# Four pairs of projection tiles per head by one level of Strassen's scheme, with quarter sums of x in DRAM

## What is computed

```python
xn = rmsnorm(x, norm_gain)
proj = xn @ w_in                          # (tokens, 1024) x (1024, 4616)
gb, gc, hc, zc, q, k, v, o, zm, ig, fg = split(proj)   # 512 each; ig, fg: 4
yc, conv_new = short_conv(gc * hc, conv_buf, conv_w)   # 3 taps over time
y_conv = gb * yc * silu(zc)
h, state = mlstm(q, k * 128 ** -0.5, v, ig + b_i, log_sigmoid(fg + b_f), state)
h = head_rmsnorm(h) * mh_norm_gain
y_m = h * sigmoid(o) * silu(zm)
out = concat(y_conv, y_m) @ w_out
y = rmsnorm(x + out, final_norm_gain)     # and the new states
```

## Time and profile before

| | |
|---|---|
| time, median of 3 runs | 1104.06 us (1102.57 to 1105.48) |
| span of the profiled execution | 1100.9 us |
| time not in that span, against the median | 3.2 us |
| TensorE busy | 1061.1 us (96%), 7180 matmuls |
| VectorE, ScalarE, GpSimd busy | 540.9, 340.7, 257.9 us |
| DMA | 108.74 MB, mean 99 GB/s |

### The profile page before, as it was taken

How to read it: one execution, slowest core, us unless ns; L and a number is a source line. 1 busy time by engine, 2 the same in 40 slices (tenths; PEclk the granted TensorE clock), 3 DMA queues, 4 the chain that set the end, 5 groups by cost and what they waited for, 6 DMA issues and landing times. The chain is left out here.

```text
span 1100.9 us, 17978 instructions
## 1 busy us (share of the span) xinstructions
PE 1061.1 (96%) x7180; PEld 602.0 (55%) x7180; DVE 540.9 (49%) x1008; ACT 340.7 (31%) x672; POOL 257.9 (23%) x333
## 2 busy tenths in 40 slices
PE   3999999999999999999999999999999999999995
PEld 3655546565666555656665556566655555444442
DVE  5786664556553434575534345655332323434333
ACT  6636434243402232434022324340213131111111
POOL 5012313021211323212113232121111121542422
PEclk9999999999999999999999999999999999999998
DMA  9484532033200322342003224310212062365651
GB/s 243 135 182 78 132 86 49 24 107 101 89 22 17 96 63 77 93 110 89 21 17 96 64 77 120 102 32 22 93 43 86 25 220 91 108 223 205 233 201 77
DMA packets 124184, 108.74 MB, mean 99 GB/s; under 512 B 42384, under 2 KB 109092, under 8 KB 124100
## 3 DMA queue, kind: packets, MB, share of 16 engines
q1 hardware_dynamic: 88192, 68.83, 22.0%
q0 software_dynamic: 7600, 25.03, 6.2%
q10 hardware_dynamic: 28308, 13.73, 4.8%
HBM read 65.43 MB, written 33.41 MB: 90 GB/s over the span
## 5 line engine op out<-in xcount | busy, mean ns | idle before, releaser
L800 PE MATMUL bank<-xTh,Wh 128*128 128x512 f16 (+2 forms) x1304 | 421.2, 342 | 5.7 <-DVE Wl L163 5.7
L801 PE MATMUL bank<-xTl,Wh 128*128 128x512 f16 (+2 forms) x1304 | 423.9, 342 | 0.0
L802 PE MATMUL bank<-xTh,Wl 128*128 128x512 f16 (+2 forms) x1304 | 423.6, 342 | 0.0
L802 PEld LDWEIGHTS bank<-xTh,Wl 128*128 128x128 f16 x1304 | 129.2, 99 | 120.3 <-issue 0.7
L800 PEld LDWEIGHTS bank<-xTh,Wh 128*128 128x128 f16 x1304 | 129.2, 99 | 113.4 <-DVE Wl L163 6.0
L801 PEld LDWEIGHTS bank<-xTl,Wh 128*128 128x128 f16 x1304 | 129.3, 99 | 108.8 <-issue 2.4
L809 PE MATMUL bank<-Wh,xTh 128*128 128x128 f16 x544 | 92.8, 219 | 0.6 <-DVE ysum L163 0.6
L811 PE MATMUL bank<-Wh,xTl 128*128 128x128 f16 x544 | 92.8, 219 | 0.0
L810 PE MATMUL bank<-Wl,xTh 128*128 128x128 f16 x544 | 92.8, 219 | 0.0
L163 ACT ACTIVATE tz<-bank 128x512 f32<-128x512 f32 x32 | 19.1, 598 | 148.4 <-PE bank L802 147.7
L672 POOL TENSOR_TENSOR ysumst<-ysum,ysumst 128x1024 f16<-128x1024 f32 x16 | 34.1, 2130 | 105.5 <-ACT ysumst L163 105.5
(11 more groups left out here) (336 smaller groups left out, 1520.5 us busy)
## 6 DMA issues: line engine op xcount, KB each, us to landing
wst<-in_w_in ACTq DMA_DIRECT2D x23, 512.0 KB, 3.9
xs<-in_x_prompt SPq DMA_DIRECT2D x22, 512.0 KB, 4.3
y_ops<-ysumst POOLq DMA_DIRECT2D x16, 512.0 KB, 3.2
w_ops<-xs SPq DMA_DIRECT2D x16, 448.0 KB, 4.5
wst<-in_w_in SPq DMA_DIRECT2D x13, 512.0 KB, 5.5
out<-xs POOLq DMA_DIRECT2D x11, 512.0 KB, 2.9
Wh<-y_ops SPq DMA_DIRECT2D x12, 448.0 KB, 3.6
Wl<-y_ops SPq DMA_DIRECT2D x12, 448.0 KB, 4.4
```

The lines of the kernel that those rows point to most:

```text
L800: mm(out, wh[:, k, :], xh, start=(k == 0), stop=False)
L801: mm(out, wh[:, k, :], xl, start=False, stop=False)
L802: last = mm(out, wl[:, k, :], xh, start=False, stop=(k == KT - 1))
```

## The change

**Products.** In heads 1 to 3, K and Q, GC and HC, ZC and GB, O and ZM form four pairs. A pair of one block is a 2 x 2 problem: two halves of D (four K tiles each), two tiles, two halves of the block's tokens (256 each). Instead of eight half products, seven are done (strassen_product: 4 K tiles x 3 matmuls of 256 columns), on quarters and on sums of quarters of x and W. Seven weight operands of a pair lie in Wp[p] (OP_11 ... OP_T2), four sums of x quarters of a block in one buffer xsum (X_S2, X_S1, X_S3, X_S4). The products go, in this order, into four slots (half banks of PB0, PB1, T0, N1): first, second, third and fourth slot, then three more that accumulate on top of what VectorE has written back into the first, third and fourth (p1_ready, u4_ready, c22_ready). VectorE does five steps of 256 columns a pair (second_sum, quarter_22, fourth_sum, quarter_12, quarter_21), ScalarE two (first_copied, first_quarter). V stays as it was, and now comes first in a block (values). The mixed tokens' second tile of each pair is made from three operands, 36 matmuls of 80 columns instead of 24. Head 0 is computed tile by tile as before. The 128 ** -0.5 of the keys is now folded into the exponents.

**x.** Head 0 stores the split x of each block to DRAM (store_x, to x_ops); heads 1 to 3 load it per block into one of two regions xreg[0] and xreg[1], one block ahead (load_a). The four sums of a block (high and low parts) are computed once, from rows of x that are loaded again, in eight passes of 512 KB: two in head 0, six in blocks (1,0), (1,1) and (1,2) (SUMS_AT). A pass: rows loaded by SyncE (load_sum_rows), scaled by ScalarE (sums_norm), four sums of 512 on GpSimd (sum_rows), two high halves on ScalarE (sum_rows_high), a low half on VectorE (sum_rows_low), DMA transposes and two stores to x_sums by SyncE (turn_sums). load_sums brings the four sums of the next block (512 KB each) into xsum, at the end of SyncE's list for a block.

**Weights.** load_raw brings the raw tiles of the next head on SyncE's queue (seven in its block 2, two in block 3); VectorE scales them (raw_gain), ScalarE makes high halves (pair_high, pair_sums_high), VectorE and GpSimd low halves (pair_low, pair_sums_low), GpSimd the sums (pair_first_sum, pair_sums).

**Moved.** The slabs of w_out go to blocks (2,1), (2,2), (3,1), (3,2). In VectorE's list sum_rows_low, or the second output_low, is the last of such a block. The output stage loads its operands late, into memory of xreg and Wp that comes free. Several small buffers (gain, junk) share memory.

The core of the diff, all in the engine lists and their helpers:

```diff
+PAIRS = [(K, Q), (GC, HC), (ZC, GB), (O, ZM)]
+NP = len(PAIRS)
+HALF = BT // 2
+W_ORDER = [V, K, Q, GC, HC, ZC, GB, O, ZM]
+OP_11, OP_21, OP_T3, OP_22, OP_T4, OP_T1, OP_T2 = range(7)
+WOPS = 7
+X_S2, X_S4, X_S3, X_S1 = range(4)
+XREG = 2 * KT * BT
 STATES_IN = DB * H + DB * 2 * H
...
+SUMS_AT = {(1, 0): (2, 3), (1, 1): (4, 5), (1, 2): (6, 7)}
...
+            def load_sums(g, b):
+
+                m = v_of(g, b)
+                sp.wait_ge(xq_out, xq_out_0 + (32 * 2 * (b + 1) if g == 1 else 32 * NQ))
+                src = x_sums[b, :, :].rearrange("p (r s h k t) -> p r (s h) k t", r=2, s=2, h=2, k=KT)
+                dst = xsum.rearrange("p r s h k t -> p r (s h) k t")
+                for op, product in ((X_S2, 2), (X_S1, 3), (X_S3, 4), (X_S4, 6)):
+                    if m:
+                        sp.wait_ge(s_prod, 7 * (NP * m - 1) + product)
+                    elif op == X_S2:
+                        sp.wait_ge(tile_done, 3 * NT)
+                    r, k = op // 2, slice(op % 2 * (KT // 2), (op % 2 + 1) * (KT // 2))
+                    sp.dma_start(dst[:, r, :, k, :], src[:, r, :, k, :]).then_inc(xs_in[op], 16)
...
+            for g in range(1, H):
+                for b in range(NB):
+                    m = v_of(g, b)
+                    if m + 1 < (H - 1) * NB:
+                        load_a(*divmod(m + 1 + NB, NB))
+                    for i, q in enumerate(SUMS_AT.get((g, b), ())):
+                        if b == 0 and i == 0:
+                            sp.wait_ge(wt_low, 3)
+                        load_sum_rows(q)
+                        turn_sums(q)
+                    if (g, b) in SLAB_FIRST:
+                        first_slab = SLAB_FIRST[g, b]
+                        for slab in (first_slab, first_slab + 1):
+                            load_slab(slab)
+                        for slab in (first_slab, first_slab + 1):
+                            store_slab(slab)
+                    if g < H - 1 and b == NB - 2:
+                        sp.wait_ge(wt_low, NP * g)
+                        if g == 1:
+                            sp.wait_ge(xq_out, xq_out_0 + 32 * NQ)
+                        else:
+                            sp.wait_ge(wo_out, 32 * SLABS // 2)
+                        load_raw(g + 1, V, K, Q, GC, HC, ZC, GB)
+                    if g < H - 1 and b == NB - 1:
+                        sp.wait_ge(wv_low, wv_low_0 + g + 1)
+                        load_raw(g + 1, O)
+                        sp.wait_ge(wt_low, NP * g + 1)
+                        load_raw(g + 1, ZM)
+                    if m + 1 < (H - 1) * NB:
+                        load_sums(*divmod(m + 1 + NB, NB))
+
+            last = unit_of(H - 1, NB - 1, 0)
             sp.wait_ge(wo_out, 32 * SLABS)
...
+            def pool_heads(g, b):
+                before = divmod(nth(g, b) - 1, NB)
+                ahead = b == NB - 1 and g < H - 1
+                if b == 0:
+                    pair_sums(g, 2)
+                    pair_first_sum(g, 3)
+                    pair_sums_low(g, 2)
+                store_y(*before, 1)
+                y_operands(*before)
+                if b == 0:
+                    pair_sums(g, 3)
+                if ahead:
+                    pair_first_sum(g + 1, 0)
+                if (g, b) in SUMS_AT:
+                    sum_rows(SUMS_AT[g, b][0])
+                store_sums(*before)
+                if b == 0:
+                    pair_sums_low(g, 3)
+                if ahead:
+                    pair_sums(g + 1, 0)
+                if b == 1:
+                    store_states(g)
+                if (g, b) in SLAB_FIRST:
+                    output_sums(SLAB_FIRST[g, b])
+                if b == 0:
                     pool.wait_ge(mx_ms, g + 1)
                     pool.tensor_tensor(hm[:, 4:5], hm[:, 3:4], halves[0:MIX, 0:1], ALU.pow).then_inc(mx_rs, 1)
-                if first and b == 0:
-                    x_power(9)
+                if ahead:
+                    pair_first_sum(g + 1, 1)
+                    pair_sums_low(g + 1, 0)
+                store_y(g, b, 0)
                 if b == 0:
                     store_mixed(g, 0)
-                if b == 1:
-                    pool.wait_ge(mx_states, g + 1)
-                    dst = c_s[:, bass.ds(g, 1), :, :].rearrange("b h d v -> d (b h) v")
-                    pool.dma_start(dst, cs[:, :, 0:P]).then_inc(cs_out, 16)
-                if (g, b) in SLAB_FIRST:
-                    output_sums(SLAB_FIRST[g, b])
-                store_y(g, b, 0)
                 if (g, b) in SLAB_FIRST:
                     output_sums(SLAB_FIRST[g, b] + 1)
-                if first and b == 0:
-                    x_power(10)
-                pool.wait_ge(h_ms, nth(g, b) + 1)
-                pool.tensor_tensor(hrs[:, :], hms[:, :], halves[:, :], ALU.pow).then_inc(h_rs, 1)
+                if ahead:
+                    pair_sums(g + 1, 1)
+                head_power(g, b)
                 if b == 0:
                     store_mixed(g, 1)
+                if (g, b) in SUMS_AT:
...
+            def strassen_product(unit, part_x, op, slot, start):
+
+                p = unit % NP
+                for k in range(KT // 2):
+                    wh, wl = Wp[p][:, op, 0, k, :], Wp[p][:, op, 1, k, :]
+                    mm(slot_bank[slot], wh, part_x(0, k), start=(start and k == 0), stop=False, skip_group_check=not start)
+                    mm(slot_bank[slot], wh, part_x(1, k), start=False, stop=False, skip_group_check=not start)
+                    last = mm(slot_bank[slot], wl, part_x(0, k), start=False, stop=(k == KT // 2 - 1), skip_group_check=not start)
+                last.then_inc(s_prod, 1)
...
+            def pair_block(g, b, p, between):
+
+                unit, m = unit_of(g, b, p), v_of(g, b)
+                x = x_block(g, b)
+                first, second, third, fourth = range(4)
+
+                def quarter(row, half):
+                    return lambda part, k: x[:, part, half * (KT // 2) + k, row * HALF:(row + 1) * HALF]
+
+                def sums(op):
+                    return lambda part, k: xsum[:, op // 2, part, :, op % 2 * (KT // 2) + k, :]
+
+                if b == 0:
+                    pe.wait_ge(wb_low, wb_low_0 + w_pairs(g, p) + 1)
...
+                    pe.wait_ge(wt_low, w_pairs(g, p) + 1)
+                between(0)
+                use_slot(first, unit)
+                strassen_product(unit, quarter(0, 0), OP_11, first, True)
+                between(1)
+                use_slot(second, unit)
+                if p == 0:
+                    pe.wait_ge(xs_in[X_S2], xs_in_0[X_S2] + 16 * (m + 1))
+                strassen_product(unit, sums(X_S2), OP_T2, second, True)
+                between(2)
+                use_slot(third, unit)
+                if p == 0:
+                    pe.wait_ge(xs_in[X_S1], xs_in_0[X_S1] + 16 * (m + 1))
+                strassen_product(unit, sums(X_S1), OP_T1, third, True)
+                between(3)
+                use_slot(fourth, unit)
+                if p == 0:
+                    pe.wait_ge(xs_in[X_S3], xs_in_0[X_S3] + 16 * (m + 1))
+                strassen_product(unit, sums(X_S3), OP_T3, fourth, True)
+                between(4)
+                pe.wait_ge(p1_ready, unit + 1)
+                strassen_product(unit, quarter(0, 1), OP_21, first, False)
+                between(5)
+                pe.wait_ge(u4_ready, unit + 1)
+                if p == 0:
+                    pe.wait_ge(xs_in[X_S4], xs_in_0[X_S4] + 16 * (m + 1))
+                strassen_product(unit, sums(X_S4), OP_22, third, False)
+                between(6)
+                pe.wait_ge(c22_ready, unit + 1)
+                strassen_product(unit, quarter(1, 1), OP_T4, fourth, False)
+                between(7)
+
+            def pe_heads(g, b):
+                n, m = nth(g, b), v_of(g, b)
+
+                def values():
...
+                def values():
+
+                    if b == 0:
+                        pe.wait_ge(wv_low, wv_low_0 + g)
+                    pe.wait_ge(xa_in[m % 2], 16 * (m // 2 + 1))
+                    if m:
+                        pe.wait_ge(slot_free[1], 5 * m)
+                    else:
+                        pe.wait_ge(p_free[1], NT * NB // 2)
+                    for c in range(CH):
+                        last = value_product(PB[1][:, c * P:(c + 1) * P], block_x(g, b, c, c + 1))
+                    last.then_inc(v_done, 1)
...
+                def in_keys(k):
+                    if k == 2:
+                        pe.wait_ge(n_free, n)
+                        pe.wait_ge(s_free, n * 3)
+                        transposed(g, eh, t0(g, b, "hT"))
+                    if k == 3 and b == 1:
+                        states_round(g, b, 1)
+                    if k == 4 and b == 0:
+                        mixed_tile(g, b, K)
+                    if k == 6:
+                        arguments(g, b)
+                    if k == 7 and b == 0:
```

(49 more changed lines are left out.)

1394 lines of the change are left out of this document (1014 added, 380 removed).

## The result

The changed kernel takes 1445.88 us (1442.46 to 1454.95, 4 runs) against 1103.49 us for the kernel before in the same series: 1.3116 times as long, 95% interval 1.3074 to 1.3158. The profiled execution has a span of 1443.7 us. So the change makes the kernel 342 us slower; forecast were 215 us, and the range ended at 1390.

A forecast was written before the change was run, and what follows sets the result against it. TensorE, 96% busy, was taken as the bound. Span 1100.9 - 52.2 array time + 130 x sums + 81.5 head starts + 20 head 0 + 26 clock + 10 contention = 1316.2, forecast 1319 us; range 1195 to 1390.

The forecast's parts named there:

- last term: GpSimd and VectorE contending side by side, plus VectorE's long list before a head's end: 10 us, bounds 0 and 25.
- clock: TensorE falls to half rate after idling: 2 us for each of 13 long waits, 26 us.
- x sums: Seven waits before blocks of heads 1 to 3 for late-loaded x sums: 130 us, bounds 95 and 160.
- last block of head 0: Waits from ScalarE's rows, VectorE's weight loads and sums handed between engines: about 20 us, bounds 5 and 30.
- head starts: TensorE waits in blocks (g,0) for values, mixed K and mixed GC: 81.5 us, bounds 50 and 100.
- Array time: TensorE in heads 1 to 3: 336 matmuls of 256 columns replace 192 of 512 per block; -52.2 us overall.
- the link I named: Head starts: ScalarE's high halves for pairs 2 and 3 precede its copy of values; 17.5 us late, heads 2 and 3.
- As a sum this fits: Plain blocks: VectorE's work rises to about 29 of 46.7 us, ScalarE and GpSimd below half; only order does not fit.
- (c): Rival: lists lock into each other further than followed, each wait moving the next; over 1390, say 1420 us; chance 0.1.
- Output stage: Kernel's end: its weights load during the last two pairs and first products; cost 0, at most 5 us.

The follow-up runs named there:

- Runs 1: Changed kernel with the next block's x sums loaded ahead of the seven weight loads in SyncE's list, blocks (1,2) and (2,2); 1429.45 us against 1445.88.
- runs 2: Changed kernel with the next block's x sums loaded ahead of the second w_out slab's stores, in the four slab blocks; 1391.22 us against 1445.88.
- 3: Changed kernel with the second pass over x left out in (1,0), (1,1), (1,2), results wrong; 1371.6 us against 1445.88.
- run 4: Changed kernel with ScalarE's copies of values and mixed K put ahead of high halves at head starts; 1446.9 us against 1445.88.
- run 9: kernel 7 with VectorE's cn updates earlier and, in (1,1) and (1,2), ScalarE's row scaling later and x sums loaded ahead of rows; 1266.59 us.
- kernel 10: kernel 7 with GpSimd's weight sums and low halves for heads 2 and 3 cut to 2 of 128 columns, results wrong; 1226.5 us.
- run 11: kernel 10 with GpSimd waiting for two 16-byte DMAs ahead of each group of sums and each pair's low halves, results wrong; 1255.52 us.
- kernel 7: Changed kernel with head-start lists reordered, passes earlier in own buffers, x sums ahead of slab stores and weights, V/K gains and head 0 row scaling later; 1273.55 us.
- 8: Changed kernel with dummy 256-column matmuls ahead of each of the seven x-sum waits; 1463.49 us against 1445.88.

## Why the prediction was wrong

The direction was right, and so were the long waits and their places; the size was short by 127 us (1319 against 1446). By the terms of the sum: last term (contention, VectorE's long list) 62 us, clock 33, x sums 18, last block of head 0 8, head starts 6. Point by point:

**Array time: right.** In (3,1) a matmul of 256 columns follows another after 109.2 ns on average (325 steps), forecast 109; 192 of 512 columns at 215.9 gave way to 336: 4.8 us a block. TensorE's busy time shows less of it: without what half clock added (60.4 us after, 1.7 before) it fell by 41 us, from 1059.4 to 1018.5, and in (3,1) from 53.26 to 49.28. A matmul of 256 columns is on record for 0.27 us, while the next can follow after 0.109, so 0.16 us of a wait can lie hidden in busy time. The missing 11 us are short waits, not array time: with every matmul priced at the median step of its form the kernel after has 53 us less.

**x sums: right, somewhat short.** Forecast 20, 21, 34, 10, 25, 10, 10; measured 23.9, 24.5, 37.6, 12.0, 25.9, 12.2, 12.4. Together 148.4 for 130. Runs 1, 2 and 3 take each away by its named cause. What was missing before (1,1): the V tile starts at 411.02, which is T, and GpSimd's power ended at 419.03, so at T + 8.0 and not T + 4.5, in part because VectorE stood 2.7 us at a mixed result that its list has ahead of the means; the rest of the chain, 23.4 us from there to the load's landing, was forecast at 20.8 and 1.4 for the first pass.

**Head starts: right in size, and in the cause only in part.** v 22.6 and 21.5 for 17.5 and 17.5, kfm 3 x 10.5 for 3 x 10, gcm 3 x 3.9 for 3 x 3.5; 87.2 for 81.5; the 6 us forecast for v in head 1 did not come. But run 4 shows that the link I named was not what set the time: with it moved the next link, of equal length, took over.

**Last block of head 0:** four waits and the one at its end add to 28.2 us (8.0, 2.2, 6.6, 4.7, 6.7), for 20.

**The step that failed most was the last term, contention and VectorE's long list: 10 us.** What none of the terms above has comes to 72 us (342.8 + 52.2 - 148.4 - 87.2 - 28.2 - 58.7 of clock). 59 us of it can be read as waits in heads 1 to 3, 0.2 to 4.2 us each: 37 in the blocks 1 to 3 of the heads (cn 29, kw 5, to 3), and 22 beside the mixed tokens at the heads' starts (um, dp, cn and others); 11 us are the ones hidden in busy time. I had taken the pairs as covered because VectorE has 29 us of work in 46.7. "As a sum this fits" was the argument. But the updates of cn stand behind a convolution or a slab in a fixed list: in (2,1), (2,2), (3,1) and (3,2) run 9 takes the waits for them from 2.4 to 2.8 us down to 0.2 to 0.5 by their place alone. And VectorE slows beside GpSimd (runs 10 and 11, made on kernel 7). How the 72 us of the kernel after divide between the two is not shown. That VectorE's share rises only from 49% to 50% hides both: of a span 31% longer it is 721 us for 541. I had seen the slowing, in the earlier trace rows, as GpSimd's loss of 0.9 us; it was VectorE's that counted. Timelines of VectorE and GpSimd in kernel 7, start of (2,0):

```profile
617.63 2.13 DVE L200 TENSOR_SCALAR to<-to,par 128x512 f32<-128x512 f32 x1
619.80 2.49 DVE L200 SCALAR_TENSOR_TENSOR ysum<-to,ysum 128x512 f32<-128x512 f32 x1
```

```profile
617.03 4.71 POOL L982 TENSOR_TENSOR Wp<-xs,Wp 128x1024 f16<-128x1024 f32 x2
```

and the same two instructions in kernel 10, with GpSimd's cut short:

```profile
605.04 0.48 DVE L200 TENSOR_SCALAR to<-to,par 128x512 f32<-128x512 f32 x1
605.56 0.69 DVE L200 SCALAR_TENSOR_TENSOR ysum<-to,ysum 128x512 f32<-128x512 f32 x1
```

2.13 for 0.48 us and 2.49 for 0.69. GpSimd's pair of instructions ends at 621.74 (the first at 619.48), and VectorE's two end at 619.76 and 622.29, each 0.3 to 0.6 us behind one of them, nearly as if it had begun only then. The Trainium skill, "SBUF — State Buffer", Who interferes with whom, says that the one that comes second stands still until the first is done. These rows come within 0.2 us of it. By that rule the price is the rest of GpSimd's instruction, not a share of VectorE's.

**Clock: 58.7 us for 26.** From the granted clock's record TensorE was busy for 121 us at 1.2 GHz, 60.4 us lost, against 1.7 before. That is 2.2 us a stretch, so the price of 2 us was right and the count wrong: I had counted 13 waits, and there are 27 such stretches, since short waits are followed by one too. Timeline of TensorE, kernel after, block (0,3):

```profile
268.80 0.39 PE L1140 MATMUL bank<-xeven,Wp 128*128 128x512 f16 x1 [2.21 <-ACT gcs L200]
269.03 0.38 PE L1141 MATMUL bank<-xeven,Wp 128*128 128x512 f16 x1
269.24 0.40 PE L1142 MATMUL bank<-xeven,Wp 128*128 128x512 f16 x1
269.46 0.61 PE L1140 MATMUL bank<-xeven,Wp 128*128 128x512 f16 x1
...
272.42 0.61 PE L1141 MATMUL bank<-xeven,Wp 128*128 128x512 f16 x1
272.85 0.40 PE L1142 MATMUL bank<-xeven,Wp 128*128 128x512 f16 x1
```

A wait of 2.2 us, and from 269.46 on steps of 0.43 us instead of 0.22. That is the gross price. Net it was 1.1 to 1.9 us of 2.0 to 2.4 in three blocks, and nothing in a fourth (runs 2 and 8), so the 58.7 and the 72 us are not wholly independent: a faster TensorE would have met some of the other engines' waits earlier. How much of the one hides the other over the whole kernel stays open.

**Rivals.** The result lies nearest to (c), over 1390, say 1420 us, with a chance of 0.10: the lists locked into each other; run 4 is that rival in small. It had been given too little: nothing but the end of my own walk through the lists stood against it.

**Output stage:** 0 to 5 forecast. With its last wait gone the stretch from the last V tile is 214.5 us (kernel 7) against 212.2, though a K tile (5.2 us before) more of the last block now lies in it; the array time of that block fell by 4.8.

## What to carry to other kernels

Where one engine is busy 96% of the time, 5% off its work was worth nothing, because the lists that feed it had not been walked for each new hand-over; add the price of all waits first, and count those of 1 to 4 us that a total of busy time cannot show. A wait has to be traced through all lists before one position is moved: the move of a single link gave 0 us of 75, the move of all gave 47. A stand-in for an engine's work has to be timed in its place before its run is read: the DMAs of run 11 were meant to be as long as the sums, and at two places were some 8 us longer. Work put on GpSimd is not free for VectorE: here the same 99 instructions took 16 us longer beside it.

## What the runs showed of the hardware

VectorE's instructions of 512 columns in SBUF took 2.13 and 2.49 us beside GpSimd's, for 0.48 and 0.69 alone: 4.4 and 3.6 times as long. In one head's start and the end before it this came to 22 us (41.04 + 58.60 - 35.33 - 42.29), and it stayed away in kernel 11, where GpSimd waited instead of computing (35.31 and 41.81 us). After a wait of only 2.2 us TensorE ran eight matmuls at 1.2 GHz, beginning 0.7 us behind the wait. With dummy matmuls in the wait's place the granted clock stayed at 1.00 in (2,2) and (3,2). A stretch at half clock lost TensorE's matmuls 2.2 us on average (60.4 us in 27), and taking it away gave 1.1 to 1.9 us in three blocks and nothing in one. A DMA of 16 bytes that GpSimd waited for cost 1.6 to 2.1 us at most places, and 4.6 to 7.0 at the heads' starts.
